# Three moves in a two-layer streaming encoder step: the store of x behind the third weight chunk, the rounding of weights ahead of the first evacuation, and two low parts of y on VectorE

## The reference

```python
proj = x @ w_in + b_in      # [q_a k_a v_a g_a | q_b k_b v_b g_b | q_idx k_idx w_idx | r_a r_b]
y_a = stick_breaking(q_a, k_a, v_a) * silu(g_a)
sel = top_k(sum_h w_idx * relu(q_idx . k_idx))       # 128 keys for the prompt, 80 for the sample
y_b = softmax_attention(q_b, gathered k_b, v_b, bias) * silu(g_b)
merged = sigmoid(r_a) * (y_a @ w_proj_a) + sigmoid(r_b) * (y_b @ w_proj_b)
x = layer_norm(ALPHA * x + merged @ w_out)           # the next layer's x
```

## Time and profile before

| | us |
|---|---|
| median of 3 runs | 1057.68 |
| lowest and highest | 1056.74, 1057.71 |
| the profiled execution | 1056.88 |
| its span (first to last instruction) | 1055.1 |
| busy in the span: PE / DVE / ACT / POOL | 1003.9 / 606.0 / 480.1 / 498.6 |

### The profile page before, as it was taken

How to read it: one execution, slowest core, us unless ns; L and a number is a source line. 1 busy time by engine, 2 the same in 40 slices (tenths; PEclk the granted TensorE clock), 3 DMA queues, 4 the chain that set the end, 5 groups by cost and what they waited for, 6 DMA issues and landing times.

```text
span 1055.1 us, 18633 instructions
## 1 busy us (share of the span) xinstructions
PE 1003.9 (95%) x7557; PEld 919.1 (87%) x7557; DVE 606.0 (57%) x1203; ACT 480.1 (46%) x824; POOL 498.6 (47%) x334
## 2 busy tenths in 40 slices
PE   1899999999999999999998999989999999999996
PEld 1789898878899999998777899977888999999975
DVE  6659997788983101101583899987898311100137
ACT  1355435667876322223124733466688542222210
POOL 2234455544564744445434174554455474445540
PEclk9999999999999999999999999999999999999999
DMA  6531453011112224323225223211111222352312
GB/s 198 192 102 46 146 165 126 2 41 41 41 41 81 80 81 161 100 81 120 91 68 195 76 91 113 82 58 42 41 41 42 72 65 80 100 184 81 106 55 90
DMA packets 70073, 95.44 MB, mean 90 GB/s; under 512 B 4458, under 2 KB 61252, under 8 KB 69348
## 3 DMA queue, kind: packets, MB, share of 16 engines
q1 hardware_dynamic: 66068, 82.68, 24.2%
q0 software_dynamic: 3488, 10.46, 2.9%
q10 hardware_dynamic: 432, 1.11, 0.3%
HBM read 79.46 MB, written 14.78 MB: 89 GB/s over the span
## 4 chain that ended last, share of the span: by engine, by line
PE 76%; DVE 15%; DMA 3%; issue 2%; ACT 2%; POOL 2%; SPq 0%; DVEq 0%; ACTq 0%; POOLq 0%
PE ps L514 35%; PE ps L861 10%; PE ps L812 10%; DVE attn L1346 3%; PE ps L727 3%; DVE top L1343 3%; PE ps L537 2%; PE ps L748 2%; PE ps L787 2%; PE ps L766 2%; PE ps L706 2%; DVE attn L1319 2%; DMA raw<-in_w_in 2%; DVE attn L1381 1%; DVE x_nat L1235 1%
## 5 line engine op out<-in xcount | busy, mean ns | idle before, releaser
L1566 POOL TENSOR_TENSOR w_lo<-raw,w_hi 128x1024 fp32r<-128x1024 f32 (+1 forms) x116 | 283.0, 2440 | 404.6 <-ACT w_hi L912 404.5
L514 PE MATMUL ps<-xT_hi,w_hi 128*128 128x288 f32 x864 | 256.1, 296 | 0.0
L514 PE MATMUL ps<-xT_hi,w_lo 128*128 128x288 f32 x864 | 254.5, 295 | 0.0
L514 PE MATMUL ps<-xT_lo,w_hi 128*128 128x288 f32 x864 | 254.5, 295 | 0.0
L912 ACT ACTIVATE w_hi<-raw 128x1024 fp32r<-128x1024 f32 (+1 forms) x116 | 121.2, 1046 | 107.2 <-PE ps L514 72.7
L1527 DVE TENSOR_TENSOR qy<-qy,ps 128x576 f32<-128x576 f32 x32 | 24.1, 754 | 253.8 <-PE ps L514 253.8
L514 PEld LDWEIGHTS ps<-xT_hi,w_hi 128*128 128x128 f32 x864 | 162.1, 188 | 1.3 <-issue 1.1
L514 PEld LDWEIGHTS ps<-xT_lo,w_hi 128*128 128x128 f32 x864 | 162.1, 188 | 0.0
L514 PEld LDWEIGHTS ps<-xT_hi,w_lo 128*128 128x128 f32 x864 | 162.0, 188 | 0.0
L961 ACT ACTIVATE qy<-ps,bias 128x576 f32<-128x576 f32 x34 | 25.2, 742 | 126.3 <-PE ps L514 126.2
L1657 POOL TENSOR_TENSOR attn<-attn 128x1024 f32<-128x1024 f32 (+1 forms) x24 | 54.2, 2259 | 59.2 <-DVE attn L1454 59.2
(11 more groups left out here) (202 smaller groups left out, 2300.3 us busy)
## 6 DMA issues: line engine op xcount, KB each, us to landing
raw<-in_w_in SPq DMA_DIRECT2D x44, 1024.0 KB, 5.2
raw<-in_w_out SPq DMA_DIRECT2D x8, 1024.0 KB, 5.0
x_kept<-x_nat SPq DMA_DIRECT2D x2, 2560.0 KB, 11.1
x_nat<-x_kept SPq DMA_DIRECT2D x2, 2560.0 KB, 11.2
raw<-in_w_proj_a SPq DMA_DIRECT2D x8, 512.0 KB, 3.5
raw<-in_w_proj_b SPq DMA_DIRECT2D x8, 512.0 KB, 4.7
x_nat<-in_x_prompt SPq DMA_DIRECT2D x4, 512.0 KB, 7.6
out<-stage POOLq DMA_DIRECT2D x8, 256.0 KB, 4.3
```

The costliest lines, as they stand in the source:

```text
L514: last = mm(out, a, b[:, HALF * half:HALF * (half + 1)], start=(k == 0 and i == 0), stop=(k == n - 1 and i == 2))
L1566: g.tensor_tensor(lo, src, hi.bitcast(f32), ALU.subtract).then_inc(s_lo, 1)
```

## The change

The store of x is issued after chunk 2 instead of after chunk 1. On ScalarE, `head(2)` comes before `evacuate(0)`, and `head(3)` after the copy `ki_nat`. The low parts of the last two rows of y (`Y_ORDER[6:]`, rows 2 and 3) are computed by VectorE, behind its eight gate multiplications and with a semaphore of their own, and no longer by GpSimd. The waits on `s_ylo` are adapted to six instead of eight per layer.

```diff
@@ semaphores
+        s_ylo_v = sem("last_y_low_parts_by_vector")
@@ SyncE, in the loop over chunks
-                    if c == 1:
+                    if c == 2:
                         sp.wait_ge(s_x0, L * 5 + 5)
                         sp.wait_ge(s_x, L * 5 + 5)
                         sp.dma_start(x_kept, x_nat[:, :, :].rearrange("p a n -> p (a n)")).then_inc(s_kept, 16)
@@ TensorE, dense(), PR
-                            pe.wait_ge(s_ylo, L * 8 + 8)
+                            pe.wait_ge(s_ylo, L * 6 + 6)
+                            pe.wait_ge(s_ylo_v, L * 2 + 2)
@@ ScalarE, evacuate(), RA and RB
-                            act.wait_ge(s_ylo, L * 8 + (i + 1 if i < 4 else 8))
+                            act.wait_ge(s_ylo, L * 6 + (i + 1 if i < 4 else 6))
+                            if i >= 4:
+                                act.wait_ge(s_ylo_v, L * 2 + 2)
@@ ScalarE, front of a layer
+                head(2)
                 evacuate(0)
-                head(2)
                 keys_hi(0, ki_hi, s_kihi)
                 evacuate(1)
-                head(3)
                 act.wait_ge(s_kin, L + 1)
                 act_f(ki_nat[:, :, :], ps[:, 4, 0:360].rearrange("p (t c) -> p t c", t=5), ACT.Copy).then_inc(s_kinev, 1)
+                head(3)
                 queries_hi(1)
                 evacuate(2)
@@ VectorE, behind the gate multiplications
+                for n, i in enumerate(Y_ORDER[6:]):
+                    dve.wait_ge(s_yhi, L * 8 + 7 + n)
+                    v.tensor_tensor(late_y_lo[:, i, :], qy[:, y_row(i), :], late_y_hi[:, i, :].bitcast(f32),
+                                    ALU.subtract).then_inc(s_ylo_v, 1)
@@ GpSimd
                 for n in range(4):
-                    y_rest(Y_ORDER[2 * n])
-                    y_rest(Y_ORDER[2 * n + 1])
+                    if n < 3:
+                        y_rest(Y_ORDER[2 * n])
+                        y_rest(Y_ORDER[2 * n + 1])
                     if n < 3:
                         rest(N_G + A_UNITS + 2 + n)
```

## The result

The changed kernel took 1050.40 us (median of 4 runs, 1049.67 to 1050.74), the kernel before beside it 1057.23 us (1056.74 to 1057.71). The ratio is 0.9938 (95% interval 0.9926 to 0.9951): 6.8 us faster, where 1052.0 and a gain of 5.3 were forecast. In a second set of runs, beside other runs of the kernel before, the ratio was 0.9936 (0.9921 to 0.9950). The direction and the places were right.

What follows compares the result with a forecast made beforehand. The chain that ended last was 76% TensorE and 15% VectorE, with 5.12 us of TensorE pauses at the changed places. Gains of 0.64 + 3.22 + 1.46 = 5.32 us gave 1052.0 us, range 1050.6 to 1054.2.

Steps and rivals of the forecast that it cites:

- Rounding of unit 2 first: Front of layer 0: head(2) ahead of the first evacuation starts 0.64 us sooner; gain 0.64, with 0.14 of TensorE's pause left.
- The cover of the moved evacuation: Front of layer 0: evacuate(0) starts 0.95 us later and ends by 48.4, 1.2 us ahead of its reader.
- head(3) behind the copy: Front of layer 0: head(3) comes 0.46 us later behind the ki_nat copy, with 2.0 us of cover; cost nothing.
- third rival: Front of layer 1: chunk 2 not late or not released early, only head(2) and y steps work; 1054.6 us, chance 0.04.
- The store behind the chunk: Front of layer 1: chunk 2 issued without waiting for x, so dense(3) starts at 565.29 instead of 568.51; gain 3.22 us.
- the store could land sooner with chunk 2 gone: Front of layer 1: store of x, landing 13.6 us after issue with chunk 2 behind it, can land sooner; counted no later.
- The low parts of y: Before PR: VectorE computes the last two low parts, TensorE goes on without pause; gain 0.73 us per layer, 1.46 in all.
- the fear that it would be: Before PR: GpSimd's weight low part stretched by 0.64 us beside VectorE, ending at 354.9 at the latest, still in time.
- the rule that the prediction quotes: Trainium skill: VectorE with two SBUF inputs and GpSimd share ports under an exclusive lock; the later is blocked throughout the instruction.
- That the y step gives nothing: Before PR: VectorE's two low parts end no sooner than GpSimd's did, as both stretch each other; 1053.5 us, chance 0.10.
- That VectorE gives it back in the selection: Layer 1 selection: VectorE held by GpSimd's weight parts partly loses the front's gain; two added hits, 1054.8 us, chance 0.08.
- The slower one: Front: the store of x lands late and delays dense(4); 1061 us if landing 26 us after issue, chance 0.04.

Runs made afterwards that it cites:

- the order alone: Kernel before with only ScalarE's order changed (head(2) ahead of evacuate(0), head(3) behind the ki_nat copy), store of x unmoved: 1057.26 us, ratio 1.0002.
- the two edits at the start of layer 0: Changed kernel with GpSimd's low part of unit 1 delayed: 1048.75 us; additionally with the first layer_norm in VectorE's wait for the fourth row tile: 1048.03 us.

## Why the prediction was right, and where it was small

**Rounding of unit 2 first: 0.64 forecast, 0.62 by the table and 0.61 alone.** The pause left over was 0.16, forecast 0.14. The cover of the moved evacuation held. That the copies of the keys keep their times was not exact: they start 1.72 us behind the release instead of 1.58, which nothing waits for.

**head(3) behind the copy: nothing forecast, nothing found.** This holds with the chunk early. With the chunk late both moves together gave layer 1 no more than 0.29, and next to nothing without the chunk's own scatter. The prediction's third rival counted 0.64 for head(2) in that layer, so its 1054.6 was too low by that much.

**The store behind the chunk: 3.22 forecast, 3.19 found.** Both workings (the chain of starts, and the comparison with the other layer) came out, and the distances are equal in both layers: 9.77 and 9.78 us against 9.75 forecast. The shared reason was shown by taking the edits apart: 2.58 with the store alone, at most 0.29 with the order alone, 3.19 with both. The gain passed through the selection undiminished (4.97 us of lead before it, 5.10 at the end of it).

One claim beside it was wrong and cost nothing: that the store could land sooner with chunk 2 gone. It landed 13.4 us after its issue in layer 1, and 13.6 before. In the traces with chunk 2 behind it in the same queue it took 13.3 to 13.6 us there, and in those without 12.6 to 13.6, so chunk 2 took nothing from it that shows.

**The low parts of y: 1.46 forecast, 1.78 found at the first matmuls of PR, about 1.9 with their slower restart.** This is the term that was mis-sized, by 0.3 to 0.5 us in two layers. The mechanism was as written. VectorE's timeline before PR in layer 0, and GpSimd's (answering to the earlier trace rows):

```profile
351.58 3.15 DVE L1525 TENSOR_TENSOR late_y_lo<-qy,late_y_hi 128x576 fp32r<-128x576 f32 x2 [11.40 <-ACT late_y_hi L403]
```

```profile
351.05 2.40 POOL L1574 TENSOR_TENSOR w_lo<-raw,w_hi 128x1024 fp32r<-128x1024 f32 x1 [0.57 <-ACT w_hi L914]
```

The first part ends at 351.58 + 2.48 = 354.06, 0.61 us behind GpSimd's 353.45, and the second at 354.73, 1.28 behind it, near the forecast's 0.54 + 0.75. (The 0.75 was read from a multiplication with one operand in `ps`; the second subtraction took 0.75 too.)

GpSimd was not stretched, and the fear that it would be rested on a wrong reading. The prediction took the GpSimd part of 2.04 us for a first comer that VectorE slowed. It came second, as VectorE's timeline of the kernel before shows in narrow windows:

```profile
335.11 0.74 DVE L1518 TENSOR_TENSOR qy<-qy,x_nat 128x576 f32<-128x576 f32 x1
336.22 1.55 DVE L1518 TENSOR_TENSOR qy<-qy,x_nat 128x576 f32<-128x576 f32 x1 [0.37 <-ACT x_nat L1185]
```

This multiplication had begun at 335.11, 0.01 us ahead of GpSimd's part, and ended at 335.85. GpSimd ended at 337.16, 1.31 later, about what its part takes alone (1.40). The next multiplication, begun at 336.22, ended 0.61 behind GpSimd. In these rows the second comer waited and the first was not slowed, so they do not speak against the rule that the prediction quotes, as it thought.

The error of size is in what a pause costs. The bracket of a TensorE row runs from the modelled end of the last matmul (0.29 after its start) to the start of the next. In a steady stream the next starts 0.13 after the last, so 0.16 of overlap is lost too. Start to start, PR stood 357.17 - 356.14 = 1.03 behind RB1 before and stands 355.45 - 355.31 = 0.14 now: 0.89 gained, not 0.73. The second matmul follows at 0.13 instead of 0.21, another 0.08. The prediction named the overlap of 0.16 as the upper end of the term, 1.8, and did not take it; the slower second matmul it did not have.

**The rest.** 0.19 us arose ahead of the moved instructions of ScalarE: TensorE stepped at 0.24 us a matmul there until 38.3 us in the profile of before and until 38.1 after, and at 0.13 behind that. One edit could act earlier, since chunk 2 of layer 0 is issued at 21.24 instead of 37.49. But ScalarE's release comes at 45.42, 46.40 and 46.73 us in the three profiles with SyncE's old order and between 45.61 and 46.54 in the four with the new one (the two edits at the start of layer 0 and the later store left out), so this is most likely a difference between executions. That the last 0.6 us between 6.2 and 6.8 are one too is not shown, but single runs of the kernel before lay between 1055.15 and 1059.73 in the later sets.

**The rivals.** That the y step gives nothing: excluded by its pause of zero. That VectorE gives it back in the selection: excluded by the lead, and its first multiplication there took 2.18 us where it had taken 2.17. That the chunk was not late: excluded by the store alone. The slower one did not happen, but is real. The text said that a landing 22 us behind the old time of issue would cost the whole sum of 5.3 us. With the store one chunk later it landed in layer 1 at 575.6, some 22.6 us behind the last normalised row (TensorE's transposes of that row were released at 553.0), and the pause was 5.20. Start to start it cost 5.36 us, where the text's rule gives 6.0 for this landing: it let dense(4) start 5.2 us behind the landing, though its own terms (0.74 twice, 1.06 and 2.4) add up to 4.94, and 4.5 was measured. Left out were the 2.4 us of slow clock behind the pause and the same wait in layer 0, of which the text had only said that moving the store gives nothing there.

## What to carry to other kernels

Two pauses with one late transfer behind them are not two gains: follow each name up the queue until the late thing, and price the edits together. A layer that runs twice is its own control, and the distance between the same two events in both told the gain to 0.03 us before anything was built. A big transfer that waits for a late value should not stand in an in-order queue ahead of one whose data is ready, but how far it can be pushed back ends at its first reader.

## What the runs showed of the hardware that was not expected

- Behind pauses of 4.00 and 5.20 us TensorE's granted clock fell to its 1.2 GHz level, where it stayed for 5.4 us of work in both layers (matmuls of 448 columns at 0.37 us instead of 0.205) and cost 4.9 us more than the pauses themselves. Behind the pause of 2.66 us in the kernel with the order alone it did not: the granted clock was 1.00 in the windows 566 to 576 us.
- A VectorE subtraction with both operands in SBUF, asked for while GpSimd subtracts, ended 0.54 us behind GpSimd's end in the earlier trace rows and 0.61 behind it here, at 354.06. GpSimd waits likewise when VectorE was first, even by 0.01 us (2.04 instead of 1.40 us). Taking one such GpSimd instruction (2.79 us there) off the start was worth 2.08 us of VectorE's time and 1.9 of the kernel's.
- The store of 2.5 MB took 12.6 to 13.6 us in layer 1, with and without a load behind it, and 8.3 to 10.2 in layer 0. Beside it in layer 1 run the loads of the cached keys and values that GpSimd issues. In the kernel with the store one chunk later it is issued behind them and took 11.5 us, and 10.2 in layer 0, but there it also has a load just ahead of it in its queue; so that the cached keys make the difference is likely and not shown.
